# Decoder trunk with differential attention: the inverse norms of o as a row through DRAM, and o scaled in place one head later

## The reference, cut to what matters

```python
def _diff_attn(h, k, v, w_q, ..., subln, w_o, rel_bias, lambda_init):
    ...
        p = jax.nn.softmax(sc, axis=-1)
        a = p[:, :, 0] - lam * p[:, :, 1]
        return jnp.einsum('bhqk,bkhe->bqhe', a.astype(v.dtype), v)
    o = lax.map(block, (jnp.arange(nb), qb))
    o = o.transpose(1, 0, 2, 3, 4).reshape(b, s, N_HEADS, V_DIM)
    o = _rmsnorm(o, subln) * (1.0 - lambda_init)
    return o.reshape(b, s, V_WIDTH) @ w_o
```

## Time and profile before

| | us |
|---|---|
| three runs | 947.13, 948.00, 948.67 (median 948.0) |
| the profiled execution, its device time | 949.32 |
| its span in the profile | 947.5 |
| PE busy | 936.8 (99%) |
| DVE busy | 685.0 (72%) |
| ACT busy | 470.1 (50%) |
| POOL busy | 89.2 (9%) |

### The profile page before, as it was taken

One profiled execution on the slowest core, in us unless ns is written; L12 is line 12 of the kernel. 1 busy time (PEld: TensorE's weight loads), 2 busy tenths in 40 slices (PEclk: granted clock), 3 DMA queues, 4 the chain that ended last, 5 costly groups with the idle time before them and its releaser, 6 DMA issues.

```text
span 947.5 us, 11757 instructions
## 1 busy us (share of the span) xinstructions
PE 936.8 (99%) x4463; PEld 775.0 (82%) x4463; DVE 685.0 (72%) x995; ACT 470.1 (50%) x612; POOL 89.2 (9%) x70
## 2 busy tenths in 40 slices
PE   8999999999999999999999999999999999999998
PEld 6888888888888888778888878888888888888887
DVE  5876766676677679878878886767766676676685
ACT  7644343333434437777777774534434433433441
POOL 3000000100000002132222220000000000010000
PEclk9999999999999999999999999999999999999999
DMA  7328672494465543322333222235586359238635
GB/s 256 105 89 237 157 226 98 100 261 127 125 167 159 163 90 113 92 80 83 91 92 91 77 89 90 89 90 147 165 224 176 107 120 262 90 89 223 177 89 134
DMA packets 99853, 128.86 MB, mean 136 GB/s; under 512 B 3336, under 2 KB 62520, under 8 KB 99808
## 3 DMA queue, kind: packets, MB, share of 16 engines
q1 hardware_dynamic: 85632, 98.31, 31.6%
q0 software_dynamic: 14080, 29.91, 17.2%
q10 hardware_dynamic: 96, 0.02, 0.0%
HBM read 126.11 MB, written 4.74 MB: 138 GB/s over the span
## 4 chain that ended last, share of the span: by engine, by line
PE 95%; DVE 2%; issue 1%; DMA 1%; ACT 1%; SPq 0%; DVEq 0%; ACTq 0%
PE bank L1628 30%; PE bank L1630 30%; PE bank L1629 30%; PE bank L1890 1%; PE bank L1900 1%; PE bank L1929 1%; DMA work<-in_x_dram 1%; PE bank L1805 1%; DVE work L1463 0%; PE bank L1775 0%; PE bank L1739 0%; PE bank L1878 0%; PE bank L1871 0%; DVE work L1473 0%; DVE a_low_buf L1049 0%
## 5 line engine op out<-in xcount | busy, mean ns | idle before, releaser
L1628 PE MATMUL bank<-h_high_buf,w_high 128*128 128x512 f32 x640 | 252.7, 395 | 2.1 <-DVE pass_cell L1046 2.1
L1630 PE MATMUL bank<-h_high_buf,w_low 128*128 128x512 f32 x640 | 250.1, 391 | 0.0
L1629 PE MATMUL bank<-h_low_buf,w_high 128*128 128x512 f32 x640 | 249.7, 390 | 0.0
L1628 PE MATMUL bank<-w_high,a_high_buf 128*128 128x512 f32 (+1 forms) x452 | 175.9, 389 | 0.0
L1630 PE MATMUL bank<-w_high,a_low_buf 128*128 128x512 f32 (+1 forms) x452 | 175.1, 387 | 0.0
L1629 PE MATMUL bank<-w_low,a_high_buf 128*128 128x512 f32 (+1 forms) x452 | 175.0, 387 | 0.0
L1040 DVE TENSOR_TENSOR w_low<-raw,w_high 128x2048 fp32r<-128x2048 f32 (+2 forms) x58 | 123.8, 2135 | 51.2 <-ACT w_high L716 31.4
L1628 PEld LDWEIGHTS bank<-h_high_buf,w_high 128*128 128x128 f32 x640 | 120.6, 188 | 28.9 <-DVE pass_cell L1046 2.5
L1630 PEld LDWEIGHTS bank<-h_high_buf,w_low 128*128 128x128 f32 x640 | 120.4, 188 | 25.4
L1629 PEld LDWEIGHTS bank<-h_low_buf,w_high 128*128 128x128 f32 x640 | 120.7, 189 | 24.2
L725 ACT ACTIVATE work<-work 128x512 f32<-128x512 f32 x64 | 40.0, 632 | 177.9 <-DVE work L1107 177.9
(11 more groups left out here) (180 smaller groups left out, 1162.0 us busy)
## 6 DMA issues: line engine op xcount, KB each, us to landing
raw<-in_w_mlp_out_dram SPq DMA_DIRECT2D x24, 1024.0 KB, 6.8
raw<-in_w_mlp_out_dram POOLq DMA_DIRECT2D x24, 1024.0 KB, 8.5
raw<-in_w_mlp_in_dram SPq DMA_DIRECT2D x16, 1024.0 KB, 5.8
work<-in_w_mlp_out_dram SPq DMA_DIRECT2D x8, 1024.0 KB, 5.3
work<-in_w_mlp_in_dram SPq DMA_DIRECT2D x8, 1024.0 KB, 6.9
raw<-in_w_kv_dram SPq DMA_DIRECT2D x16, 512.0 KB, 4.2
xT<-in_w_mlp_out_dram SPq DMA_DIRECT2D x8, 1024.0 KB, 4.8
xT<-in_w_mlp_in_dram SPq DMA_DIRECT2D x8, 1024.0 KB, 7.0
```

The source lines that it names most:

```text
L1628: pe.matmul(acc, w_hi, m_hi, start=start, stop=False, skip_group_check=onto)
L1629: pe.matmul(acc, w_hi, m_lo, start=False, stop=False, skip_group_check=onto)
L1630: return pe.matmul(acc, w_lo, m_hi, start=False, stop=stop, skip_group_check=onto)
```

## The change: what it does

For heads m = 0 to 5 the inverse norms don't go through DVE's copy and PE's transposes any more.

- ACT's `o_copies` writes the unscaled o straight into `o_all[:, h, :]`; the tile `of` is gone. Inside the loop this address depends on h.
- A DRAM tensor `o_rstd_row` of 512 floats is new. In head h from 1 to 6, ACT issues the store of `o_rstd_buf` ([128, 4] to 512 single floats, element i*128 + p from partition p, column i) behind the high part of k. At the end of the head, behind the squares of o, it issues the load of the whole row to all 128 partitions (256 KB) into `o_rstd_bc`, which is `y_buf[:, 0, :]`.
- The waits that come with it: the store waits for `o_inverse` and, from head 2 on, for the load of the head before (`o_row_landed`); the load waits on ACT for the store to have landed (`o_row_stored`) and for the last reader of the row (`o_ready`); DVE's inverse in head h waits for the store of the head before.
- `o_norm_row(m)` on DVE multiplies `o_all[:, m, :]` by `o_rstd_bc` in place, in head m + 2, where `o_norm` of the head before stood. Both inputs are in SBUF now; one was a PSUM bank. Head 1 has none; that of m = 5 stands in head 7 behind `combine(last, 3)`.
- PE loses `turn(osq, O[3], o_spread, ...)` in heads 1 to 6, four transposes each, and waits for `o_sum` and not for `o_ready` before `values(h)`.
- Heads 6 and 7 of o (m = 6, 7) go as before, with the spread as a step of its own (`o_spreads`).
- Head 1 is written out on ACT and DVE, and the loop begins at 2.

```diff
+        o_rstd_bc = y_buf[:, 0, :]
-        of = region(3072, S)
...
+        o_row = nc.dram_tensor("o_rstd_row", (S,), F32, kind="Internal").ap()
...
             def o_copies(h, b):
                 act.wait_ge(pv_done, h + 1)
-                act.activation(of, b[:, :], ACT.Copy).then_inc(o_copied, 1)
+                dst = o_all[:, h, :] if isinstance(h, int) else o_all[:, bass.ds(h, 1), :]
+                act.activation(dst, b[:, :], ACT.Copy).then_inc(o_copied, 1)
+
+            def store_o_row(m):
+                act.wait_ge(o_inverse, m + 1)
+                act.dma_start(o_row.rearrange("(i p) -> p i", p=P), o_rstd_buf[:, :], allow_slow_non_contiguous=True).then_inc(o_row_stored, 16)
+
+            def load_o_row(m):
+                act.wait_ge(o_row_stored, 16 * m + 16)
+                act.dma_start(o_rstd_bc, o_row.rearrange("(a n) -> a n", a=1).to_broadcast([P, S])).then_inc(o_row_landed, 16)
...
                 k_high(n)
+                if not second:
+                    act.wait_ge(o_row_landed, 16 * h - 16)
+                store_o_row(h - 1)
                 bias_scale(n, (2, 3))
                 split_high_rest(U_HEAD + 2 + 2 * n)
                 if last:
                     o_high(1)
                 o_copies(h, I[3])
                 o_squares(h, I[3])
+                if not second:
+                    act.wait_ge(o_ready, h - 1)
+                load_o_row(h - 1)
...
             def o_inverses(m):
                 dve.wait_ge(o_rooted, m + 1)
                 dve.reciprocal(o_rstd_buf[:, :], o_root_buf[:, :]).then_inc(o_inverse, 1)
+
+            def o_spreads(m):
                 dve.wait_ge(o_inverse, m + 1)
                 dve.tensor_copy(osq.rearrange("p (i n) -> p i n", i=TT), ...).then_inc(o_spread, 1)
...
+            def o_norm_row(m):
+                dve.wait_ge(o_row_landed, 16 * m + 16)
+                o = o_all[:, m, :] if isinstance(m, int) else o_all[:, bass.ds(m, 1), :]
+                scale = o_rstd_bc if isinstance(m, int) else y_buf[:, 0:1, :]
+                dve.tensor_tensor(o, o, scale, ALU.mult).then_inc(o_ready, 1)
...
                 if not first:
+                    if not second:
+                        dve.wait_ge(o_row_stored, 16 * h - 16)
                     o_inverses(h - 1)
                 at_lows(h)
                 k_norm(n, I[0])
...
                     bias_scale(n, (0, 1))
-                    o_norm(h - 1, O[3])
+                    if not second:
+                        o_norm_row(h - 2)
...
             combine(last, 3)
+            o_norm_row(last - 2)
             split_low(U_WO + 1, 0)
             o_inverses(last - 1)
+            o_spreads(last - 1)
...
                 turn(ksq, I[0], k_spread, n, k_turned)
-                if not first:
-                    turn(osq, O[3], o_spread, h - 1, o_turned)
                 project(None, 0, 0, I[2], h_high_buf, h_low_buf, w_used, range(6 if first else 5, KC))
                 if not first:
-                    pe.wait_ge(o_ready, h)
+                    pe.wait_ge(o_sum, h)
                 values(h, I[3])
```

More of the change, by code:

```diff
@@ L374, in build_program @@
         o_ready = sem("o_ready")
+        o_row_stored = sem("o_row_stored")
+        o_row_landed = sem("o_row_landed")
         y_turned = sem("y_turned")
@@ L965, in first_head, with head @@
                 split_high_rest(U_HEAD + 4)
-            def head(h, last=False):
+            def head(h, last=False, second=False):
                 n = h + 1
@@ L991, in head @@
                 o_squares(h, I[3])
+                if not second:
+                    act.wait_ge(o_ready, h - 1)
+                load_o_row(h - 1)
             first_head()
-            with act.Fori(1, H - 2) as h:
+            head(1, second=True)
+            with act.Fori(2, H - 2) as h:
                 head(h)
@@ L1490, in o_norm @@
             def o_norm(m, b):
-                dve.wait_ge(o_turned, m + 1)
-                dst = o_all[:, m, :] if isinstance(m, int) else o_all[:, bass.ds(m, 1), :]
-                dve.tensor_tensor(dst, of, b[:, :], ALU.mult).then_inc(o_ready, 1)
+                dve.wait_ge(o_turned, m - (H - 3))
+                dve.tensor_tensor(o_all[:, m, :], o_all[:, m, :], b[:, :], ALU.mult).then_inc(o_ready, 1)
+            def o_norm_row(m):
[3 more added lines that the diff above has]
+                dve.tensor_tensor(o, o, scale, ALU.mult).then_inc(o_ready, 1)
             def o_low(k):
@@ L1529, in _, with head @@
             take_v(0)
-            def head(h, first, last=False):
+            def head(h, first, last=False, second=False):
                 n = h + 1
@@ L1573, in _ @@
             head(0, True)
-            with dve.Fori(1, H - 2) as h:
+            head(1, False, second=True)
+            with dve.Fori(2, H - 2) as h:
                 head(h, False)
@@ L1602, in _ @@
             o_inverses(last)
+            o_spreads(last)
             o_norm(last, O[0])
@@ L2013, in _ @@
             wo_part(U_WO + 1, 1, 0, [0])
-            turn(osq, O[3], o_spread, last_h - 1, o_turned)
+            turn(osq, O[3], o_spread, 0, o_turned)
             wo_part(U_WO + 1, 1, 0, [1])
@@ L2022, in _ @@
             wo_part(U_WO + 2, 0, 1, [0], [1, 2, 3])
-            turn(osq, O[0], o_spread, last_h, o_turned)
+            turn(osq, O[0], o_spread, 1, o_turned)
             wo_part(U_WO + 2, 0, 1, [1], [1, 2, 3])
```

## The result

The changed kernel takes 996.8 us (median of 6 runs, 994.6 to 1001.2) against 948.3 for the kernel before in the same session: a ratio of 1.051, interval 1.049 to 1.053. The forecast was 945.2 us. It is 48.5 us slower.

The account below looks back on a forecast made before the run. PE was taken as the bound, 95% of the chain that ended last. The terms -2.6 + 0.4 - 1.2 + 0.6 = -2.8 us against 948.0 gave 945.2 us, own range 944.0 to 945.9; 944.0 to 947.6 with most rivals.

Parts of the forecast that it names:

- the store's landing: ACT's load at the end of a head waits for the store; landing taken as 2.5 us, costing nothing.
- that rival: Store lands late: ACT stands before the load in six heads; above 4.5 us each microsecond is six on PE; 0.08.
- The transposes: PE in six heads: four transposes instead of eight save 0.43 us each, 2.6 us in all.
- The copy of o behind its address step: ACT, heads 2 to 5: copy starts behind a sequencer step holding the wait for `values`; 0.4 us lost.
- The lock in head 6: Head 6 to 7: DVE's low part of o gets the shared SBUF port before POOL; 1.2 us saved.
- chances of 0.45 and 0.30: 0.45 for the forecast, DVE first at the port; 0.30 for the rival that POOL stays first, 946.4 us.
- The tail in head 7: Head 7: scaling head 5's o on DVE delays later low parts, PE waits for head 4's; 0.6 us lost.

Follow-up runs that it names:

- e1_no_store: Changed kernel without the store of the inverse norms; the load reads a row of constants and nobody waits for a store: 946.2 us, ratio 0.9969.
- e7_before_store: Kernel before plus the store of 512 4-byte pieces in heads 1 to 6, nobody loading the row: 952.3 us, ratio 1.0036.
- e13_turns_kept: e1_no_store with the 24 transposes of heads 1 to 6 put back on PE, their result unused: 950.1 us, ratio 1.0010.
- the flip alone: Kernel before with DVE's take of V behind o_low(0) in head 6 instead of ahead of it: 947.4 us, ratio 0.9984.
- e16_128x8: Changed kernel storing one 8 B piece per partition, 128 side by side; the load reads a constant row but waits for the store: 947.3 us.
- e18_low4_first: e3_rows16 with take of V behind o_low(0) in head 6 and o_low(4) ahead of head 5's scaling in head 7: 944.3 us, ratio 0.9956.
- e3_rows16: Changed kernel storing one 16 B piece per partition, 128 in all, DVE reading the loaded row with a stride of four: 949.1 us, ratio 1.0002.

## Why the prediction was wrong, step by step

**The step that failed** is the store's landing: "I take 2.5 us, near the store". It is 10.0 to 11.7 us. I bounded it by the nearest rows, 1.9 and 6.7 us, both of large pieces, and the truth lay beyond the farther one; neither row had a piece below 512 B, nor 4-byte pieces that touch, and it is the touching that makes the difference: 512 B apart the same 512 pieces land after 1.8 us. "A piece of 4 bytes is next to nothing for an engine" is true (all of them done in 0.4 us) and beside the point, for the landing comes ten microseconds after that. "For it: 512 pieces, all to the same 2 KB" named the cause and got 0.08.

**The mechanism of that rival was right**: from 4.5 us on, each microsecond six times on PE. With the six distances between store and load, 65.1 us together, it gives 65.1 - 6 x 4.5 = 38 us; PE's waits are 36.3. What the rival lacked is the clock, 12 us more that come on top because PE stood (0.86 to 0.91 granted in these heads, 1.00 before them). It is somewhat more than 12: `e1_no_store` lost 1.5 us to the clock behind head 1's scores and this trace did not. The rival also lacked the other transfers, held up as well (3.5 us by themselves in `e7_before_store`); here waits and clock make up the loss, and they are no further term.

**The transposes**, 0.43 us a place: 0.44 measured. Right.

**The copy of o behind its address step**, 0.1 us a head in four heads: a head with the transposes is 24.77 us long in `e13_turns_kept` and 24.64 before, 0.13 us for this and the other small moves together. The size is right; that it is this step and not another was not tried.

**The lock in head 6**, 1.2 us saved: the flip alone gave 1.5 us by the ratio and 1.2 by the medians. DVE was first in the changed kernel, as forecast, but by less than these traces resolve; that it came out this way is luck. The changed kernel, then `e16_128x8`:

```profile
598.82 3.00 POOL L600 TENSOR_TENSOR w_low<-raw,w_high 128x1024 fp32r<-128x1024 f32 x1 [10.58 <-ACT w_high L675]
598.82 0.74 DVE L1071 SCALAR_TENSOR_TENSOR a_low_buf<-work,sub_gain,a_high_buf 128x512 fp32r<-128x512 f32 x1
```

```profile
555.42 2.37 POOL L600 TENSOR_TENSOR w_low<-raw,w_high 128x1024 fp32r<-128x1024 f32 x1 [8.88 <-ACT w_high L675]
555.44 2.90 DVE L1071 SCALAR_TENSOR_TENSOR a_low_buf<-work,sub_gain,a_high_buf 128x512 fp32r<-128x512 f32 x1
```

In the first DVE wins, in the second POOL, with the same 0.02 us between them or less. The forecast reasoned with tenths of a microsecond about something that hundredths decide; chances of 0.45 and 0.30 were about what the rows could bear.

**The tail in head 7**, 0.6 us lost at o_low(4): the wait is 0.62 us in `e1_no_store`, and `e18_low4_first`, where o_low(4) goes ahead of the scaling and PE's wait there goes with it, shows that it is this instruction.

So every term but one stood within a few tenths. Their sum, forecast -2.8 us, is -2.5 without the store by the medians, -2.9 by the ratio and -3.0 by the spans; of the executions at a mean clock of 1.000 (three against five) it is -1.6, of those at 0.998 -2.5, so it is right to about a microsecond, and the closer match is luck. The one term that failed was worth about 50.

## What to carry to other kernels

Where a change adds a wait on a path with little room, the forecast is worth no more than the duration of what is waited for: if no row has a transfer of that shape, its upper bound is not the slowest row at hand, and a mechanism that multiplies (six heads here) deserves a far larger chance. Don't store a small row as single 4-byte pieces side by side: one piece of 16 B per partition and a strided read of 0.4 us more cost far less than 4-byte pieces in the wanted order. And let the engine that issued a store go on: the load belongs on a queue whose engine has nothing behind it, or where the landing is long past. When two versions differ by a microsecond or two, compare executions with the same granted clock.

## What the runs showed of the hardware that I had not expected

- A store of 128 pieces of 4 B that touch lands after 8.9 us, one of 128 pieces of 8 B that touch after 2.8, and 512 pieces of 4 B after 4.4, 3.1, 2.2 and 1.8 us at 8, 16, 64 and 512 B apart.
- While such a store is under way, other queues' transfers stand as well: Q's weights land after 9.5 us instead of 6.7 by the median of the run.
- DVE's multiplication of 128x512 takes 1.09 us instead of 0.68 when its second input in SBUF is read with a stride of 16 B (`e3_rows16`).
- PE's stops of 5 to 7 us in six heads cost a third as much again in granted clock as in waiting: 12.2 against 36.3 us.
- A stop of PE of 2.0 to 2.1 us, the same in all traces, is followed by a granted clock of 1.00 in five of the nineteen and by a while at 0.50 in fourteen; that puts 1.5 us of chance, in one trace more, into single spans.
- With POOL first, DVE's scaling of the bias by a column (one tile in SBUF) stood too: 2.95 us instead of 0.81 in `e3_rows16`.
